# Stick-breaking attention rebuilt in units of two heads, with one PSUM bank for projection tiles

## The chip, the cores and the metric

One core of a Trainium2 chip runs one execution of a whole encoder block. The metric is device time in microseconds, lower is better. PE is the matrix engine, PEld its weight load, DVE the vector engine, ACT the scalar engine, POOL the GpSimd engine, SP the engine that here only issues DMAs. PSUM is the accumulator memory: 8 banks of 128 partitions x 512 fp32 values.

## The reference

A layer takes x (1024 tokens x 1024 features). The part that the change touches is one of two branches of the mixing sub-layer:

```
h = modulate(rmsnorm(h_res, pre_mix_g[l]), sh1, sc1)
proj = h @ w_in[l]            # q_s, k_s, v_s: 8 heads x 64 features; a_s: 1024 gate logits
z = jnp.einsum('bthd,bshd->bhts', q[:, t0:t1], k[:, :t1]) * scale
valid = s_idx[None, :] < t_idx[:, None]
log_1m = jnp.where(valid, -jax.nn.softplus(z), 0.0)
log_stick = lax.cumsum(log_1m, axis=3, reverse=True) - log_1m
a = jnp.where(valid, jnp.exp(jax.nn.log_sigmoid(z) + log_stick), 0.0)
outs.append(jnp.einsum('bhts,bshd->bthd', a, v[:, :t1]))
...
mixed = (jax.nn.sigmoid(a_r) * (ret @ w_ret_branch[l])
         + jax.nn.sigmoid(a_s) * (sb @ w_sb_branch[l]))
```

Each attention weight is thus sigmoid(z) times the product of sigmoid(-z) over all valid keys to its right. Retention, the output projection and a feed-forward layer follow. Six vectors of 1024 modulate the layer; each is silu(c) times a 1024 x 1024 matrix ("ada"). Two of them are needed at once, four later.

## The kernel before, in words

Every projection is done in three fp32r matmuls per chunk (high x high, high x low, low x high, lines 539 to 541 and 478 to 480): each operand is split into a high and a low part. The weights stream in as *pieces* of 256 columns. SP loads the two halves of a piece into `raw`; POOL splits them into `w_hi` and `w_lo` (lines 389, 391), in one of two slots, once PE has finished with what lay there; a piece is two halves.

The work before the feed-forward layer runs in stages. In the **stick stage** a loop of `STICK_G` = 2 turns does two pairs of heads each: 16 projection tiles (q and k tiles of 128 features x 512 tokens, v tiles of 128 tokens x 256 features, 8 chunks of 3 matmuls each; `stick_tile`), then `stick_pair` twice. A pair's step s takes query block i = s // 2 and head h = s % 2 of the pair, over all its (i + 1) x 128 keys at once: PE computes the scores (`scores`: 64-row operands, since a head has 64 features) into two banks and adds the mask with a matmul (L560); ACT writes sigmoid(z) to `sg` (L923) and sigmoid(-z) to `uu` (L924); DVE scans `uu` into running products from the right (L1285) and multiplies them into `sg` (L1287); PE transposes the result block by block (`weights_transposed`, L570); ACT copies it to `aT` (L929); PE multiplies with v (`times_v`, L582). v is stored with zeros beside it, so that each head's product fills 128 output partitions, its own 64 and zeros. DVE splits the result (L1292, L1294).

The order is written out by hand on each engine. On PE a step is scores(s), a part of a projection tile, transposes of step s - 2, the rest of that tile, times_v of s - 3; the table `STICK_BESIDE` says which tile stands beside which step: the first eight steps of a turn's first pair have one, the first six of its second pair too, steps after them none. Tiles of a turn's start stand alone, ahead of the pair. DVE also does the four later ada vectors there, between the scans: 64 multiply-adds over 512 columns (`ada_step`, L1267, L1269) out of `raw`, and PE sums them over partitions (`ada_row`, L592).

The **gate stage** follows, g = 0 and 1: eight tiles of 8 chunks (`piece_T`, sigmoid on ACT, L950) and eight of 4 chunks that multiply by w_sb (evicted by DVE, L1335). Then come retention, merge, output projection and feed-forward.

The changed functions of all five engines stand here as they were.

## Time and profile before

| | |
|---|---|
| runs | 1976.05, 1965.62, 1970.85 us; median 1970.85 |
| profiled execution, its own time | 1968.33 us |
| its span, first to last instruction | 1966.5 us |
| mean granted clock of PE | 0.957 of full speed |
| PE busy | 1792.9 us, 91% |
| DVE, ACT, POOL busy | 925.6, 521.7, 668.8 us |

A busy share is the share of the span in which an engine had an instruction in work. Matmuls overlap: each record is longer than the distance to the next one, so costs of PE are read from the distance between two starts. The granted clock is 1.0 at 2.4 GHz and 0.5 at 1.2 GHz. An entry such as "PE ps L570 <- DVE sg L1287" says that PE stood idle before an instruction of line 570 until DVE had finished one of line 1287.

### The profile page before, as it was taken

The page shows a single profiled execution, that of the slowest core. Times are in us where ns is not written, and L with a number is a line of the kernel's source. Part 1 is how long each engine was busy: PE and PEld are TensorE (multiplying, and loading weights), DVE is VectorE, ACT ScalarE, POOL GpSimd, SP SyncE. Part 2 cuts the span into 40 slices and gives each one's busy share as a digit, 9 for nine tenths or more (in the row PEclk, how much of TensorE's full clock was granted, in tenths as well). Part 3 has the DMA queues.
Part 4 walks back from the last instruction along what each step waited for, and adds up shares of the span by engine and source line. Part 5 has one row for each costly group of instructions (what it writes and reads, how often), then busy time and mean ns, then how long its engine had stood idle before and what let it go on. Part 6 is the DMA issues. An engine that isn't in the chain of part 4 may idle for free.

```text
span 1966.5 us, 25526 instructions
## 1 busy us (share of the span) xinstructions
PE 1792.9 (91%) x9648; PEld 1513.2 (77%) x9648; DVE 925.6 (47%) x1321; ACT 521.7 (27%) x833; POOL 668.8 (34%) x283
## 2 busy tenths in 40 slices
PE   1799889979999998999999997589999999999998
PEld 1677677767889897988788797567888888888886
DVE  6574837492105455454311326647436263453616
ACT  2333413341001212111100113342333333233332
POOL 4020132014333331313333476334543544445320
PEclk8799988999999999999999998799999999999999
DMA  8020313031113111101211144302021120211103
GB/s 313 12 97 11 96 35 107 1 97 52 46 35 140 44 38 33 44 25 43 110 62 43 43 160 141 139 33 86 22 64 43 43 68 27 75 43 43 60 31 146
DMA packets 38086, 135.15 MB, mean 69 GB/s; under 512 B 5864, under 2 KB 6760, under 8 KB 37488
## 3 DMA queue, kind: packets, MB, share of 16 engines
q1 hardware_dynamic: 30320, 109.29, 17.2%
q10 hardware_dynamic: 7680, 24.65, 3.4%
q8 instruction: 62, 1.02, 0.2%
q14 instruction: 24, 0.20, 0.0%
HBM read 121.33 MB, written 12.60 MB: 68 GB/s over the span
## 4 chain that ended last, share of the span: by engine, by line
PE 79%; DVE 12%; issue 4%; ACT 2%; POOL 2%; DMA 0%; DVEq 0%; POOLq 0%; SPq 0%; ACTq 0%
PE ps L478 15%; PE ps L479 15%; PE ps L480 15%; PE ps L820 5%; PE ps L821 5%; PE ps L822 5%; PE ps L539 3%; DVE uu L1285 3%; PE ps L540 3%; PE ps L541 3%; PE ps L582 2%; PE ps L699 1%; DVE sg L1238 1%; DVE qk L1415 1%; PE ps L570 1%
## 5 line engine op out<-in xcount | busy, mean ns | idle before, releaser
L389 POOL TENSOR_TENSOR w_hi<-raw,zero 128x1024 fp32r<-128x1024 f32 x80 | 164.9, 2062 | 833.7 <-DMA raw<-wstream 367.0
L478 PE MATMUL ps<-r_hi,w_hi 128*128 128x512 f32 x640 | 254.5, 398 | 23.1 <-issue 20.3
L479 PE MATMUL ps<-r_lo,w_hi 128*128 128x512 f32 x640 | 254.1, 397 | 0.0
L480 PE MATMUL ps<-r_hi,w_lo 128*128 128x512 f32 x640 | 252.7, 395 | 0.0
L478 PE MATMUL ps<-w_hi,a_hi 128*128 128x256 f32 x768 | 222.4, 290 | 20.6 <-DVE qkT L1421 9.1
L479 PE MATMUL ps<-w_lo,a_hi 128*128 128x256 f32 x768 | 217.6, 283 | 0.0
L480 PE MATMUL ps<-w_hi,a_lo 128*128 128x256 f32 x768 | 217.3, 283 | 0.0
L391 POOL TENSOR_TENSOR w_lo<-raw,w_hi 128x1024 fp32r<-128x1024 f32 x80 | 206.9, 2587 | 6.3
L417 POOL TENSOR_TENSOR w_lo<-w,w_hi 128x1024 fp32r<-128x1024 f32 x39 | 101.3, 2598 | 249.6 <-ACT w_hi L1070 249.6
L1551 DVE TENSOR_TENSOR m<-m,ps 128x512 f32<-128x512 f32 x224 | 146.3, 682 | 71.9 <-PE ps L822 71.6
L478 PEld LDWEIGHTS ps<-w_hi,a_hi 128*128 128x128 f32 x768 | 149.1, 194 | 23.1 <-POOL w_hi L389 10.3
L478 PEld LDWEIGHTS ps<-r_hi,w_hi 128*128 128x128 f32 x640 | 121.7, 190 | 51.2 <-issue 20.5
L820 PE MATMUL ps<-w_hi,f_hi 128*128 128x512 f32 x392 | 155.9, 398 | 4.2 <-issue 4.2
L821 PE MATMUL ps<-w_lo,f_hi 128*128 128x512 f32 x392 | 155.7, 397 | 0.0
L822 PE MATMUL ps<-w_hi,f_lo 128*128 128x512 f32 x392 | 155.5, 397 | 0.0
L480 PEld LDWEIGHTS ps<-w_hi,a_lo 128*128 128x128 f32 x768 | 148.9, 194 | 0.0
L479 PEld LDWEIGHTS ps<-w_lo,a_hi 128*128 128x128 f32 x768 | 148.6, 193 | 0.0
L480 PEld LDWEIGHTS ps<-r_hi,w_lo 128*128 128x128 f32 x640 | 121.7, 190 | 28.0
L479 PEld LDWEIGHTS ps<-r_lo,w_hi 128*128 128x128 f32 x640 | 121.7, 190 | 26.4
L1285 DVE TENSOR_TENSOR_SCAN uu<-uu 128x128 f32<-128x128 f32 (+7 forms) x64 | 100.2, 1566 | 67.7 <-ACT uu L924 67.6
L1544 DVE TENSOR_TENSOR f_lo<-hid,f_hi 128x1024 fp32r<-128x1024 f32 x35 | 48.7, 1392 | 149.0 <-ACT f_hi L1097 149.0
L417 POOL TENSOR_TENSOR w_lo<-raw,w_hi 128x1024 fp32r<-128x1024 f32 x32 | 77.6, 2433 | 99.3 <-ACT w_hi L1070 98.9
(223 smaller groups left out, 3509.2 us busy)
## 6 DMA issues: line engine op xcount, KB each, us to landing
raw<-wstream SPq DMA_DIRECT2D x112, 512.0 KB, 3.6
raw<-ada_rows SPq DMA_DIRECT2D x32, 512.0 KB, 3.5
w<-wstream SPq DMA_DIRECT2D x32, 512.0 KB, 3.5
ada_s<-ada SPq DMA_DIRECT2D x8, 1024.0 KB, 18.5
xs<-x SPq DMA_DIRECT2D x2, 2048.0 KB, 11.7
m_dram<-m1s ACTq DMA_DIRECT2D x1, 4096.0 KB, 12.5
...
```

Source lines behind the costliest of these rows:

```text
L389: nc.gpsimd.tensor_tensor(w_hi[:, slot, part], raw[:, h, :], zero[:, 0:1].broadcast_to([P, RAW]), ALU.add).then_inc(w_split, 1)
L391: nc.gpsimd.tensor_tensor(w_lo[:, slot, part], raw[:, h, :], w_hi[:, slot, part].bitcast(f32), ALU.subtract).then_inc(w_split, 1)
L417: return nc.gpsimd.tensor_tensor(out_, in0, in1, op)
L478: nc.tensor.matmul(outp, lh, rh, start=(k == 0), stop=False)
L479: nc.tensor.matmul(outp, lh, rl, start=False, stop=False)
L480: last = nc.tensor.matmul(outp, ll, rh, start=False, stop=(k == chunks - 1))
L539: nc.tensor.matmul(outp, hi, r_hi_, start=start, stop=False)
L820: nc.tensor.matmul(banks[:, t, :], fh, wh, start=(start and c == 0), stop=False, skip_group_check=not start)
L821: nc.tensor.matmul(banks[:, t, :], fh, wl, start=False, stop=False, skip_group_check=not start)
L822: last = nc.tensor.matmul(banks[:, t, :], fl, wh, start=False, stop=(c == 1), skip_group_check=not start)
L1285: V.tensor_tensor_scan(prod, prod, prod, 1.0, ALU.mult, ALU.bypass).then_inc(scan_done, 1)
L1551: V.tensor_tensor(dst, dst, bank, op).then_inc(ff_ev, 1)
```

## The change

- **Units.** The 64 head-steps become 48 *units* of both heads of a pair: query block i against at most four key blocks. Blocks 0 to 3 are one unit each, blocks 4 to 7 two: first the four blocks at the right end (`diagonal`, with the mask), then the i - 3 others, whose scan begins with the product that the first left (a copy of one column, `pad`). A pair has 12 units, its widths (keys per head) are 128, 256, 384, 512, then 512 four times paired with 128, 256, 384, 512.
- **Scores.** The six matmuls of a unit alternate between the heads: operand rows 0 to 63 and 64 to 127, written to two neighbouring banks. Banks 0, 1 and 2, 3 alternate from unit to unit.
- **One sigmoid for both heads** over two banks, sigmoid(-z) first; one copy for both heads' transposes; one multiply for both on DVE, two scans.
- **Products with v.** v has no zeros beside it. Each matmul has 64 columns of v for its stationary operand; head 0 writes output partitions 0 to 63 and head 1 writes 64 to 127 of the same bank, alternately.
- **Projection tiles.** All 32 go beside units, over all four pairs, and so do the first four gate tiles; apart from the first two they have one bank, so a tile waits until the one before it is evicted (for q and k tiles until DVE's low part). `qk_hi`, `qk_lo` are doubled.
- **PE's order in a step U**: transposes of U - 2, scores of U, tiles, times_v of U - 2.
- **Result of the products**: ACT copies it to `sbt_f` (32 copies), DVE splits it in eight wide instructions after the last unit, behind which `ada_step` and the gate tiles of 4 chunks stand.
- **Ada vectors** go from the stick stage to the gate stage, with a ring of three buffers of their own; ACT evicts and issues their rows. DVE waits for the last of these rows before retention.
- **Weight pieces** are split in straight code, each when the last tile of the piece two before it is done. The loop of two turns is gone on every engine.

Of the tables (they are 4 and 9 lines) two lines are shown. Other entries of `STICK_BESIDE` say for instance that unit 14 has chunks 3 to 7 of tile 15 (k of pair 1) and unit 15 all of tile 16 (v, second half of the heads).

```diff
+UNITS = tuple(u for i in range(T) for u in ([(i, 0, i + 1, True)] if i < 4 else [(i, i - 3, i + 1, True), (i, 0, i - 3, False)]))
+N_UNITS = len(UNITS)
+ALL_UNITS = 4 * N_UNITS
+FIRST_UNIT = tuple(k for k, u in enumerate(UNITS) if u[3])
+LAST_UNIT = tuple(k for k, u in enumerate(UNITS) if u[1] == 0)
...
+STICK_TILE = ([("q", 0, 0), ("k", 0, 0)] +
+              [("v", 0, t) for t in range(4)] + [("q", 0, 1), ("k", 0, 1), ("v", 0, 4), ("v", 0, 5), ("q", 1, 0), ("v", 0, 6), ("k", 1, 0), ("v", 0, 7)] +
...
+    0: ((2, 0, 8), (3, 0, 8)), 1: ((4, 0, 8), (5, 0, 8)), 2: ((6, 0, 8),), 3: ((7, 0, 8), (8, 0, 8)), 4: ((9, 0, 8),),
...
+            return ps[:, n, :] if n < 2 else ps[:, 7, :]
+
+        def z_banks(U, w):
+
+            return ps[:, 2 * (U % 2):2 * (U % 2) + 2, 0:w]
...
+            def ada_rows_in(lo, hi):
+
+                for m in range(lo, hi):
+                    if m >= ADA_RING:
+                        sp.wait_ge(ada_acc, m - ADA_RING + 1)
+                    sp.dma_start(ada_r[:, m % ADA_RING, :], ada_rows[m, :, :]).then_inc(ada_row_in[m % ADA_RING], 16)
+
+            for n in range(1, PC_GATE + 3):
+                piece_in(n)
+            ada_rows_in(0, 6)
+            piece_in(PC_GATE + 3)
...
+            for n, last in ((2, ("k", 0, 1)), (3, ("v", 0, 7)), (4, ("k", 1, 1)), (5, ("k", 2, 1)), (6, ("v", 1, 7)), (7, ("k", 3, 1))):
+                piece(n, n + 1, n % 2, TL_STICK + TILE_AT[last] + 1)
...
+                hi, lo = qk_hi[G % 2], qk_lo[G % 2]
+                for n, (a, b) in enumerate(((hi, hi), (lo, hi), (hi, lo))):
+                    for h in range(2):
+                        rows_ = slice(64 * h, 64 * h + 64)
+                        last = nc.tensor.matmul(z_banks(U, w)[:, h, :], a[rows_, 0, i * P:(i + 1) * P], b[rows_, 1, b0 * P:b1 * P],
+                                                start=(n == 0), stop=(n == 2 and not diagonal))
...
+                for b in range(b0, b1):
+                    for h in range(2):
+                        half = slice(h * SB_DH, (h + 1) * SB_DH)
+                        last = nc.tensor.matmul(px[half, 2, 0:P], vs[:, g, b, sub, half],
+                                                aT[:, h, (b - b0) * P:(b - b0 + 1) * P],
+                                                start=(k in FIRST_UNIT and b == b0), stop=(k in LAST_UNIT and b == b1 - 1))
...
+                    if n >= 3:
+                        pe.wait_ge(*((ev_act, EA_STICK + n) if STICK_TILE[n - 1][0] in "va" else (qk_low, LOW_AFTER[n])))
...
+            for U in range(ALL_UNITS + 2):
+                if U >= 2:
+                    weights_transposed(U - 2)
+                if U < ALL_UNITS:
+                    scores(U)
+                for n, k0, k1 in STICK_BESIDE.get(U, ()):
+                    stick_tile(n, k0, k1)
+                if U >= 2:
+                    times_v(U - 2)
...
+                if g:
+                    piece_T(n, g % 2, a_hi, a_lo, lambda j: (ev_dve, ev - 3 + j))
+                    ada_row(1)
+                    piece_T(n + 1, 1 - g % 2, a_hi, a_lo, lambda j: (ev_act, ea + j + 1))
+                    ada_row(2)
+                else:
+                    piece_T(n + 1, 1, a_hi, a_lo, lambda j: (sg_done, 2 * ALL_UNITS))
+                    pe.wait_ge(sbt_split, 8)
                 piece_T(n + 2, g % 2, sbt_hi, sbt_lo, lambda j: (ev_act, ea + j + 5) if j < 4 else (ev_dve, ev + j - 3),
                         chunks=4, cols=HALF, order=tuple((m, th) for m in range(4) for th in range(2)))
+                ada_row(3 * g)
...
+            for U in range(ALL_UNITS + 3):
+                if U >= 3 and (U - 3) % N_UNITS in LAST_UNIT:
+                    G, k = divmod(U - 3, N_UNITS)
+                    i = UNITS[k][0]
+                    act.wait_ge(av_done, T * G + i + 1)
+                    nc.scalar.activation(sbt_f[:, G, i * P:(i + 1) * P], px[:, 2, 0:P], ACT.Copy).then_inc(sbt_ready, 1)
+                if 2 <= U < ALL_UNITS + 2:
+                    _, b0, b1, _ = UNITS[(U - 2) % N_UNITS]
+                    w = (b1 - b0) * P
+                    act.wait_ge(at_tr, U - 1)
+                    nc.scalar.activation(aT[:, :, 0:w], px[:, 0:2, 0:w], ACT.Copy).then_inc(at_ready, 1)
+                if U < ALL_UNITS:
+                    _, b0, b1, _ = UNITS[U % N_UNITS]
+                    w = (b1 - b0) * P
+                    act.wait_ge(z_done, 2 * U + 2)
+                    nc.scalar.activation(uu[:, U % 2, :, HALF - w:HALF], z_banks(U, w), ACT.Sigmoid, scale=-1.0).then_inc(sg_done, 1)
+                    nc.scalar.activation(sg[:, U % 2, :, 0:w], z_banks(U, w), ACT.Sigmoid).then_inc(sg_done, 1)
+                for n, _, k1 in STICK_BESIDE.get(U, ()):
+                    if k1 == KC:
+                        high(n)
...
+            def row_out(v):
+
+                act.wait_ge(ada_mm, 2 + v + 1)
+                for hv in range(2):
+                    nc.scalar.activation(acc[0:1, v, hv, :], px[0:1, 2 * (v % 2) + hv, :], ACT.Copy).then_inc(ada_ev, 1)
+                act.wait_ge(ada_ev, 2 + 2 * v + 2)
+                act.dma_start(mods[v:v + 1, :], acc[0:1, v, :, :].rearrange("p a n -> p (a n)")).then_inc(mods_out, 16)
...
+                for h in range(2):
+                    run = uu[:, slot, h, HALF - w:HALF if diagonal else HALF + 1][:, ::-1]
+                    dve.wait_ge(sg_done, 2 * U + 1)
+                    V.tensor_tensor_scan(run, run, run, 1.0, ALU.mult, ALU.bypass).then_inc(scan_done, 1)
+                dve.wait_ge(scan_done, 2 * U + 2)
+                if k not in LAST_UNIT:
+                    V.tensor_copy(uu[:, 1, :, HALF:HALF + 1], uu[:, 0, :, 0:1]).then_inc(pad_set, 1)
+                    pads += 1
+                dve.wait_ge(sg_done, 2 * U + 2)
+                V.tensor_tensor(sg[:, slot, :, 0:w], sg[:, slot, :, 0:w], uu[:, slot, :, HALF - w + 1:HALF + 1], ALU.mult).then_inc(a_done, 1)
+                for n, _, k1 in STICK_BESIDE.get(U, ()):
+                    if k1 == KC and STICK_TILE[n][0] in "qk":
+                        low(n)
...
+            dve.wait_ge(sbt_ready, 4 * T)
+            for G in range(4):
+                V.tensor_copy(sbt_hi[:, G, :], sbt_f[:, G, :]).then_inc(sbt_split, 1)
+                dve.wait_ge(sbt_split, 2 * G + 1)
+                V.tensor_tensor(sbt_lo[:, G, :], sbt_f[:, G, :], sbt_hi[:, G, :].bitcast(f32), ALU.subtract).then_inc(sbt_split, 1)
...
+                for m in range(14, 24) if g else range(6):
+                    ada_step(m)
                 for j in range(8):
+                    ada_step((24 if g else 6) + j)
...
+            dve.wait_ge(mods_out, 16 * 4)
```

**On PE, a head-step of 640 keys before** (pair 0, block 4; a step without a tile beside it). L570 are the transposes, L582 the products with v, the others the scores, L560 the mask.

```order
L570 MATMUL ps<-id_f,sg 128x128 x4
L580 REGISTER_ALU
L582 MATMUL ps<-aT,vs 128x128 x4
L554 REGISTER_ALU
L539 MATMUL ps<-qk_hi 128x512
L540 MATMUL ps<-qk_lo,qk_hi 128x512
L541 MATMUL ps<-qk_hi,qk_lo 128x512
L539 MATMUL ps<-qk_hi 128x256
L540 MATMUL ps<-qk_lo,qk_hi 128x256
L541 MATMUL ps<-qk_hi,qk_lo 128x256
L560 MATMUL ps<-msk_b,id_b 128x128
```

And the change's unit 11 (pair 0, block 7, its four left key blocks; also without a tile). L591 are the transposes, L575 the scores of both heads, L608 the products.

```order
L608 MATMUL ps<-aT,vs 64x128 x8
L591 MATMUL ps<-id_f,sg 128x128 x6
L575 MATMUL ps<-qk_hi 128x512 x2
L575 MATMUL ps<-qk_hi,qk_lo 128x512 x2
L575 MATMUL ps<-qk_lo,qk_hi 128x512 x2
L608 MATMUL ps<-aT,vs 64x128 x6
L591 MATMUL ps<-id_f,sg 128x128 x8
```

The scores of one head have become those of two, each pass twice in a row on different halves of the rows, and the products with v are 64 wide and follow the transposes of their own unit at a distance of the scores (and of the tile, where there is one).

**On DVE before**, between two scans of pair 0 (queries of block 3), stand the ada multiply-adds and the split of the result:

```order
L1285 SCALAR_TENSOR_TENSOR uu<-uu 128x512
L1286 REGISTER_ALU
L1287 TENSOR_TENSOR sg<-sg,uu 128x512
L1290 REGISTER_ALU
L1292 ISA
L1292 COPY sbt_hi<-ps 128x128
L1293 REGISTER_ALU
L1294 REGISTER_ALU
L1294 TENSOR_TENSOR sbt_lo<-ps,sbt_hi 128x128
L1269 SCALAR_TENSOR_TENSOR acc<-raw,silu_c,acc 128x512
L1265 REGISTER_ALU
L1269 SCALAR_TENSOR_TENSOR acc<-raw,silu_c,acc 128x512
```

and the change's DVE, units 20 to 22 (pair 1, blocks 6 and 7; L1295 the scans, printed by the form of their instruction; L1301 the multiply, L1276 the low part of a q or k tile):

```order
L1295 SCALAR_TENSOR_TENSOR uu<-uu 128x512 x2
L1298 COPY uu<-uu 128x2
L1301 TENSOR_TENSOR sg<-sg,uu 128x1024
L1276 SCALAR_TENSOR_TENSOR qk_lo<-ps,qk_hi 128x512
L1295 SCALAR_TENSOR_TENSOR uu<-uu 128x385 x2
L1301 TENSOR_TENSOR sg<-sg,uu 128x2x384
L1295 SCALAR_TENSOR_TENSOR uu<-uu 128x512 x2
L1298 COPY uu<-uu 128x2
L1301 TENSOR_TENSOR sg<-sg,uu 128x1024
```

Nothing but scans, multiplies and low parts stands there now.

**On PE around unit 15 of the change**, with what each row waits for: scores and mask of unit 15, then the first matmul of tile 16, the first tile that uses piece 4.

```order
L575 MATMUL ps<-qk_hi 128x512 [waits sg_done]
L575 MATMUL ps<-qk_hi 128x512
L575 MATMUL ps<-qk_hi,qk_lo 128x512 x2
L575 MATMUL ps<-qk_lo,qk_hi 128x512 x2
L581 MATMUL ps<-msk_b,id_b 128x128 x2
L558 MATMUL ps<-w_hi,a_hi 128x256 [waits qk_low,w_split]
L559 MATMUL ps<-w_lo,a_hi 128x256
L560 MATMUL ps<-w_hi,a_lo 128x256
```

Piece 4 goes into the slot of piece 2, whose last tile is tile 15, the one directly ahead of tile 16.

## Rows read from the trace of the kernel before

**Rows 1.** The page, section 4: the whole chain by engine, share of the span.
```profile
PE 79%; DVE 12%; issue 4%; ACT 2%; POOL 2%; DMA 0%; DVEq 0%; POOLq 0%; SPq 0%; ACTq 0%
```

**Rows 2.** Stretches: us, then busy of each engine (instructions), granted clock, DMA, GB/s.
```profile
74.40:266.30 191.90, 168.55 (x1002) 139.55 (x1001) 125.00 (x151) 70.56 (x120) 32.60 (x12) 0.93 0.18 56
266.30:457.90 191.60, 170.70 (x1000) 141.28 (x1000) 119.48 (x139) 64.69 (x113) 32.52 (x12) 0.92 0.20 61
457.90:590.80 132.90, 132.90 (x585) 109.21 (x585) 12.25 (x20) 9.58 (x16) 43.37 (x21) 1.00 0.16 48
```

**Rows 3.** Waits of PE, 74 to 458 us: total us, times, longest.
```profile
PE ps L570 <- DVE sg L1287: 33.4, 17, 8.1
```

**Rows 4.** Timeline of PE, end of pair 1: start, us, line, tile, count.
```profile
247.97 1.97 PE L570 MATMUL ps<-id_f,sg 128*128 128x128 f32 x8 [8.14 <-DVE sg L1287]
...
261.32 2.00 PE L592 MATMUL ps<-acc,ones 128*1 128x512 f32 x4
266.31 0.47 PE L539 MATMUL ps<-a_hi,w_hi 128*128 128x512 f32 x1 [2.99 <-issue]
```

**Rows 5.** Timeline of DVE in that place, a scan of 1,024.
```profile
240.72 4.42 DVE L1285 TENSOR_TENSOR_SCAN uu<-uu 128x1024 f32<-128x1024 f32 x1
```

**Rows 6.** Timeline of ACT: eviction of a v tile, then of a gate tile.
```profile
91.68 0.39 ACT L909 ACTIVATE vs<-ps 128x256 f32<-128x256 f32 x1 [2.33 <-PE ps L541]
...
469.21 0.60 ACT L950 ACTIVATE m1s<-ps 128x512 f32<-128x512 f32 x1 [4.89 <-PE ps L480]
```

**Rows 7.** Timeline of PE, one head, 640 keys: scores, mask, transposes, products.
```profile
132.60 0.49 PE L539 MATMUL ps<-qk_hi 64*128 64x512 f32 x1
132.94 0.39 PE L540 MATMUL ps<-qk_lo,qk_hi 64*128 64x512 f32 x1
133.17 0.39 PE L541 MATMUL ps<-qk_hi,qk_lo 64*128 64x512 f32 x1
...
133.78 0.23 PE L560 MATMUL ps<-msk_b,id_b 128*128 128x128 bf16 x1
133.85 0.61 PE L570 MATMUL ps<-id_f,sg 128*128 128x128 f32 x4
134.29 1.06 PE L582 MATMUL ps<-aT,vs 128*128 128x128 f32 x8
135.28 0.50 PE L539 MATMUL ps<-qk_hi 64*128 64x512 f32 x1
```

**Rows 8.** Timeline of PE in retention: records of 128 rows, then of 64.
```profile
642.92 0.61 PE L721 MATMUL ps<-vr,st_sb 128*128 128x128 f32 x4
643.46 0.49 PE L725 MATMUL ps<-state,qkT 64*128 64x128 f32 x4
643.79 0.39 PE L688 MATMUL ps<-qkT 64*128 64x128 f32 x4
```

**Rows 9.** Groups by form, 74 to 458 us, DVE then ACT: busy, mean ns.
```profile
L1269 DVE SCALAR_TENSOR_TENSOR acc<-raw,silu_c,acc 128x512 f32<-128x512 f32 x56 | 50.1, 894 | 1.1
...
L1310 DVE SCALAR_TENSOR_TENSOR qk_lo<-ps,qk_hi 128x512 fp32r<-128x512 f32 x16 | 10.8, 683 | 22.7 <-ACT qk_hi L912 22.7
L1285 DVE TENSOR_TENSOR_SCAN uu<-uu 128x512 f32<-128x512 f32 x8 | 9.8, 1222 | 5.1 <-ACT uu L924 5.1
...
L1287 DVE TENSOR_TENSOR sg<-sg,uu 128x512 f32<-128x512 f32 x8 | 5.5, 691 | 0.3
...
L924 ACT ACTIVATE uu<-ps 128x1024 f32<-128x1024 f32 x8 | 8.2, 1019 | 0.0
```

**Rows 10.** Groups of POOL, 72 to 458 us: busy, mean ns.
```profile
L391 POOL TENSOR_TENSOR w_lo<-raw,w_hi 128x1024 fp32r<-128x1024 f32 x12 | 35.4, 2954 | 0.9
...
L389 POOL TENSOR_TENSOR w_hi<-raw,zero 128x1024 fp32r<-128x1024 f32 x12 | 29.8, 2487 | 338.6 <-DMA raw<-wstream 338.6
```

**Rows 11.** Nine stretches of PE at the low clock: the third, and the sum.
```profile
242.80:253.00 10.20, 4.96 (x22) 0.50 0.39 127
...
sum 54.50, PE 42.67; mean PE 4.74
```

403 lines of the change are left out of this document (156 added, 247 removed), and 7 rows, old and new, of the table STICK_BESIDE.

## The prediction, made before the changed kernel ran

> **What bounds the kernel now.** I read the chain of waits first: PE carries 79% of it, DVE 12% [rows 1]. So a change pays where it shortens PE's own work or a wait of PE. Then the stretches of the stages the change touches [rows 2]: the stick stage runs from 74.4 to 457.9 us, 383.5 us, and PE is busy 168.6 + 170.7 = 339.3 of them: it stands idle 44.2 us. The gate stage behind it is solid PE, 132.9 of 132.9 us. In the stick stage 33.4 us of the idle time stand before the transposes, which wait for DVE's multiply, 17 times [rows 3]. The longest such wait, 8.1 us, is at the end of a pair [rows 4], where no projection tile stands beside the heads, and where a scan of 1,024 took 4.42 us [rows 5] while POOL split weights; 1.22 us for 512 [rows 9] would let one expect 2.4. After such waits the granted clock is at 0.50, the 1.2 GHz level, for 3.4 to 10.2 us: nine stretches, 54.5 us in all, with 42.7 us of PE work in them [rows 11], which cost half of that, 21 us.
>
> **Prices on PE**, from distances between starts at full clock. A q, k or gate tile (24 matmuls): 0.60 + 4.89 = 5.49 us from eviction to eviction; a v tile: 0.39 + 2.33 = 2.72 us [rows 6]. A score pass of 512 keys 0.23 us, the first one 0.34, so 0.11 for the entry; mask 0.07; one transpose 0.44 / 4 = 0.11 us; products with v 0.99 us for four blocks of one head, eight records [rows 7]. Four ada records 2.0 us [rows 4].
>
> Check on the stage before: 16 x 5.49 + 16 x 2.72 = 131.4; scores 216 passes of 512 x 0.23 + 64 x 0.18 = 61.2; 288 transposes 31.7; 288 blocks of products 71.3; ada rows 4 x 2.0 = 8.0. Sum 303.6, with 44.2 idle and 21 for the clock 369. The other 14 us (5% of the work) are short matmuls that cost more than their share.
>
> **The change, part by part.**
>
> *Scores.* Two heads alternate on the two halves of the rows. Retention already does this: four records on all 128 rows took 643.46 - 642.92 = 0.54 us, four on alternating halves 0.33 us [rows 8], which is two pairs at 0.11 and an entry of 0.1. So the halves run side by side. 108 passes x 0.23 + 48 entries x 0.11 + 32 masked units x 0.15 = 34.9 instead of 61.2 us. Bounds: 34.9, and 24.8 more if fp32r passes (retention's are fp32) do not pair.
>
> *Products with v.* The halves are now halves of the output partitions, one bank. No row shows that. Bounds: all of it serial, 71.3 us, or paired, 35.7. I take 35.7, because the nearest row [rows 8] pairs. The Trainium skill, TensorEngine Tiling (Array Packing), section Theoretical Speedup, allows up to twice the rate for 64 columns or fewer; no run here shows it.
>
> *Change of array shape.* Going from full rows to half rows cost 0.11 us [rows 7], once a unit in my sum. The Trainium skill, same page, section Key Properties, says that a change of tiling mode drains the engine. With products in half columns a unit has four changes of shape, 192 in all; at the row's 0.11 each the other 144 would add 16 us. My sum leaves them out since the row behind the scores (L560) and the transposes show no such gap; it is a rival below.
>
> *Tiles.* 16 + 4 x 5.49 and 16 x 2.72: 153.3 us; the four gate tiles (22.0) leave the gate stage. Transposes 31.7 as before.
>
> PE's work: 153.3 + 34.9 + 31.7 + 35.7 = 255.6, with 4% for short forms 265 us.
>
> *Waits of PE left in the stage.* (a) Scores of unit 0 wait for the low part of k: drain 0.2 + 0.60 + 0.68 [rows 6, 9] = 1.5. (b) One tile bank: v after v within a unit waits for drain and eviction, 0.6, twice; a tile behind a q or k tile within a unit (units 3, 13, 25, 37) 1.5; where DVE does the low part only behind its own scans, three or four times up to 2. Together 13. (c) Piece 4: it is split only when tile 15 is done, and tile 16 is the next one. A piece is 2 x (2.49 + 2.95) = 10.9 us on POOL [rows 10]; between the two tiles PE has about 1.6 us of other work: 9.3. Pieces 2 and 5 have 11 to 12 us of PE work in between, and the others more: nothing, or 2 each if DVE slows POOL. (d) After unit 47: sigmoid 1.02, two scans 2.44, multiply 1.4, copy 1.02 against some 3 us of PE work: 3.3. Sum 27.
>
> *Clock.* The 9.3 us wait should be followed by 10.2 us at the low level as in rows 11, this time full of tiles: 5; the short waits another 4. Sum 9.
>
> Stage: 265 + 27 + 9 = 301 us, for 383.5.
>
> *DVE, ACT, POOL.* Per pair DVE has 18 x 1.22 of scans, 18 x 0.69 of multiplies, four low parts of 0.68 [rows 9]: 37 us, 150 for four pairs, at most 33 more if every microsecond of the six pieces halves it. ACT: three instructions a unit, nine times 1.02 each per pair [rows 9]: 110 us, with evictions and 32 small copies 140. Both lie beside PE's 265. Within a unit of 512 with half a tile PE has about 5.7 us, DVE 3.9: PE stays last. If the pairing failed, PE would only be further behind.
>
> *Gate stage.* 132.9 - 22.0 + 8.0 (ada rows) = 118.9. DVE gets 64 multiply-adds here, 0.89 us each [rows 9], 57 us, plus 16 multiplies of 0.69 and the split of the result (eight instructions of 1,024, at most 2 x 0.69 each, 11 us): about 79 in 119. Nothing on the path: the split has four tiles (22 us) before the first use. It would cost where a 2.75 us tile stands against 1.8 + 0.69 of DVE while POOL works; three banks of lead, 8 us, cover the 5 us of delay. Without them 5 us per turn. On SP the ada loads stand behind the piece loads and these behind POOL's splits; three rows are in flight before DVE starts, and a turn has 44 us for at most 18 rows: 0, or a few us. Retention starts with DVE waiting for the last ada row: sum, copy, DMA, some 5 us, against four tiles of 2.72 in four banks: 0. The loop's return (2.99 us, [rows 4]) was in the idle time.
>
> **Sum.** 301 + 118.9 against 383.5 + 132.9: -96.5 us. The profiled execution took 1968.33 us: 1871.8. The median of the runs is 2.5 us above it; I say **1873**.
>
> **The rivals.**
> 1. *Products do not pair.* +36 us of PE work, of which some 5 fill waits: 1904. For: no row for column halves, both write one bank. Against: rows 8. Chance 0.2.
> 2. *Shape changes cost on every side.* +16: 1889. The Trainium skill's drain rule (above) would give this; the trace has the entry and not the way back. Chance 0.1.
> 3. *Scores do not pair*, alone or with the products: 1898 or 1927. Chance 0.05.
> 4. *Slower: alternating halves drain each other.* If each of 288 score and 576 product records had to wait out the tail of the one before (0.39 long at a distance of 0.23: 0.16), that is +138 on top of the 61 for no pairing: 2070. It decides from (96.5 - 61) / 864 = 0.04 us per record. Rows 8 speak plainly against it for rows, nothing does for columns. Chance 0.03.
> 5. *Weights and low parts stall PE more than I count* (pieces 2 and 5, POOL slowed by scans, bank 7 behind DVE): +15: 1888. Chance 0.12.
> That the change does no work that it removes is excluded by the order of the instructions; only the clock could take the gain back, by 20 at most.
>
> **How the numbers follow.** Main case 0.5, 1873, itself 1855 to 1890 (waits 15 to 35, clock 4 to 15, short forms 0 to 15). The range 1850 to 1908 takes in rivals 1, 2 and 5. Faster by over 0.5% (about what a measurement can tell from no change): all cases but the fourth and a part of the unknown, 0.95; same 0.02; slower 0.03.
>
> **What would show it.** In the new profile: scores of both heads starting in pairs a few ns apart, products too (if their records lie 0.12 apart one by one, rival 1); stick stage near 301 us and gate near 119; one wait of PE of about 9 us before tile 16, put down to POOL; no long wait on DVE's multiply except at the end; POOL idle elsewhere; DVE busy in the gate stage without holding PE. It is wrong if the stage takes over 335 us, or if PE waits for DVE or ACT in most units.

## The result, and the profile after

The changed kernel takes 1919.12 us (median of 4 runs, 1917.12 to 1925.92), the kernel before in the same job 1968.39 us. The ratio is 0.975, with a 95% interval from 0.9711 to 0.9788: 49 us faster. The forecast was 1873 us, 96.5 us faster, with a range of 1850 to 1908. The direction was right, the size was not: half of the gain is missing, and the time lies outside the range. Of the runs of e3_rows below, one (2048.67 us, at a granted clock of 0.83 against 0.95 to 0.96 in the others) was in a slower state of the chip and is left out of its median.

The profiled execution took 1925.92 us, 6.8 us above its median, so the sums below, made on it, come to 54 us missing and not 46. The three stretches of [rows 2], the last one reaching to the end, in the new trace (window, length in us, then busy of each engine with its instructions, granted clock, DMA share, GB/s):

```profile
74.60:398.60 324.00, 290.14 (x2066) 224.43 (x2064) 183.18 (x188) 139.79 (x216) 73.47 (x28) 0.96 0.08 25
398.60:531.60 133.00, 125.22 (x513) 93.64 (x513) 89.43 (x88) 10.64 (x19) 47.99 (x20) 0.95 0.47 159
531.60:1924.10 1392.50, 1320.54 (x6977) 1116.32 (x6976) 617.45 (x939) 354.19 (x551) 526.25 (x221) 0.97 0.19 65
```

and PE in the last one before, from the first matmul of retention, which is at 589.9 and not at 590.8 where the prediction cut (us, PE busy, clock, DMA share, GB/s):

```profile
589.90:1966.50 1376.60, 1301.12 (x6977) 0.97 0.20 66
```

So the 54 us stand in three places: the stick stage takes 324.0 us where 301 were forecast (+23), the gate stage 133.0 for 118.0 (+15; the forecast's 118.9 held 0.9 us of retention), and everything behind it, which the change does not touch, 1392.5 for 1376.6 (+16). The last one is the surprise: PE is busy for 19 us more with the same 6977 matmuls. (3.5 of these 16 us are the granted clock: PE was busy at the 1.2 GHz level for 42.6 us there and for 35.7 before, and half of the difference is time.)

The waits of PE in the first two stretches (total us, times, longest):

```profile
PE ps L591 <- DVE sg L1301: 12.7, 5, 5.9
PE ps L558 <- POOL w_lo L412: 8.4, 1, 8.4
PE ps L558 <- DVE qk_lo L1276: 8.0, 7, 1.5
PE ps L654 <- DVE acc L1328: 7.8, 1, 7.8
PE ps L608 <- ACT aT L937: 2.3, 2, 1.2
PE ps L575 <- DVE qk_lo L1276: 1.4, 1, 1.4
PE ps L558 <- ACT vs L917: 1.1, 2, 0.6
```

L591 is the transposes, L558 the first pass of a projection tile, L654 the ada rows, L608 the products, L575 the scores. The 33.4 us of [rows 3] have become 12.7; the wait for POOL is the one forecast before tile 16. The wait of L654 is the one in the gate stage, and was forecast as nothing; the others are 33.9 us in the stick stage.

One step in the timeline of PE at full clock: the end of the products, transposes, scores of both heads, masks, the first two passes of half a tile; then its last pass, the products and the next transposes.

```profile
282.37 0.61 PE L608 MATMUL ps<-aT,vs 128*64 128x128 f32 x8
282.91 1.09 PE L591 MATMUL ps<-id_f,sg 128*128 128x128 f32 x8
283.93 0.51 PE L575 MATMUL ps<-qk_hi 64*128 64x512 f32 x2
284.27 0.40 PE L575 MATMUL ps<-qk_hi,qk_lo 64*128 64x512 f32 x2
284.50 0.39 PE L575 MATMUL ps<-qk_lo,qk_hi 64*128 64x512 f32 x2
284.82 0.28 PE L581 MATMUL ps<-msk_b,id_b 128*128 128x128 bf16 x2
284.92 0.47 PE L558 MATMUL ps<-a_hi,w_hi 128*128 128x512 f32 x1
285.23 0.39 PE L559 MATMUL ps<-a_lo,w_hi 128*128 128x512 f32 x1
...
287.56 0.40 PE L560 MATMUL ps<-a_hi,w_lo 128*128 128x512 f32 x1
287.89 1.09 PE L608 MATMUL ps<-aT,vs 128*64 128x128 f32 x16
288.92 0.44 PE L591 MATMUL ps<-id_f,sg 128*128 128x128 f32 x2
```

Two things are to be seen. Both heads' scores of 512 keys take 0.89 us from the first to the mask (284.82 - 283.93), and both heads' products of four blocks 1.03 us (288.92 - 287.89), where one head alone took 0.99 [rows 7]: the heads seem to run side by side. And at each change of array shape something is lost on both sides: the first score pass is 0.34 from the next where the second is 0.23; the last of the three stands 0.32 before the mask; the first pass of the tile 0.31 before the second, where 0.23 is usual; the tile's last pass 0.33 before the products. In the trace of before the same can be read around [rows 7], where I read only the entry, 132.60 to 132.94. The next head's scores, at 135.28, stand 0.20 us behind the last product, where two products are 0.11 apart; and the last score pass,

```profile
133.57 0.27 PE L541 MATMUL ps<-qk_hi,qk_lo 64*128 64x128 f32 x1
```

stands 0.21 us before the mask (133.78), where two such passes are 0.11 apart.

In all, over the 48 units, the median excess at such places is 0.15 us from products to transposes, 0.20 from transposes to scores, 0.21 from scores through the mask to the tile, 0.14 from the tile to the products: 0.70 us a unit, 34 us in the stage. (A change can be preceded or followed by a change of data type here, of the bf16 mask above all; the 0.70 holds both.)

The work of PE by kind bears this out. Each record is counted to the start of the next one, without the waits, and time at the 1.2 GHz level is halved:

| PE work, us | before, by the check | before, in the trace | changed, forecast | changed, in the trace |
|---|---|---|---|---|
| Projection tiles | 131.4 | 138.7 | 153.3 | 166.3 |
| Scores and masks | 61.2 | 70.1 | 34.9 | 39.2 |
| Transposes | 31.7 | 31.3 | 31.7 | 38.5 |
| Products | 71.3 | 69.6 | 35.7 | 38.1 |
| Ada rows, in the changed kernel "short forms" | 8.0 | 7.7 | 9.4 | |
| Sum | 303.6 | 317.4 | 265 | 282.1 |

### The profile page after: what moved, and what is told of

It is laid out like the page before. It is cut to its first block, busy times and chain, and to the rows that moved or that the text cites. A ratio compares the mean times of both kernels' runs of the same rounds, so it can differ in the third digit from the quotient of the medians.

```text
span 1924.1 us, 24724 instructions
## 1 busy us (share of the span) xinstructions
PE 1758.3 (91%) x9648; PEld 1453.6 (76%) x9648; DVE 942.4 (49%) x1291; ACT 529.1 (27%) x822; POOL 667.4 (35%) x282
## 4 chain that ended last, share of the span: by engine, by line
PE 81%; DVE 11%; issue 3%; POOL 2%; ACT 2%; DMA 0%; POOLq 0%; DVEq 0%; SPq 0%; ACTq 0%
PE ps L497 15%; PE ps L499 15%; PE ps L498 15%; PE ps L829 5%; PE ps L831 5%; PE ps L830 5%; PE ps L558 3%; PE ps L559 2%; PE ps L560 2%; PE ps L591 2%; PE ps L575 2%; PE ps L608 1%; DVE uu L1295 1%; PE ps L708 1%; DVE sg L1256 1%
## 5 line engine op out<-in xcount | busy, mean ns | idle before, releaser
L1295 DVE TENSOR_TENSOR_SCAN uu<-uu 128x512 f32<-128x512 f32 (+7 forms) x96 | 105.1, 1136 | 118.4 <-ACT uu L942 118.1
L499 PEld LDWEIGHTS ps<-r_hi,w_lo 128*128 128x128 f32 x640 | 121.1, 189 | 29.0
## 6 DMA issues: line engine op xcount, KB each, us to landing
ada_s<-ada SPq DMA_DIRECT2D x8, 1024.0 KB, 18.5
m<-m_dram ACTq DMA_DIRECT2D x1, 4096.0 KB, 12.4
```

The source lines that it names most:

```text
L499: last = nc.tensor.matmul(outp, ll, rh, start=False, stop=(k == chunks - 1))
L1295: V.tensor_tensor_scan(run, run, run, 1.0, ALU.mult, ALU.bypass).then_inc(scan_done, 1)
```

## The experiments

All are edits of the changed kernel unless another is named, and each time is a median of 4 to 10 runs. "Of a0" means against the changed kernel's 1920.61 us in the first of these jobs; kernels of different jobs are compared over it, which is good to some 3 us, the before of the jobs lying between 1968 and 1974. A difference of under 5 us needs the profile too, as the next section shows.

### The changed kernel again (a0_same)

No edit.

> The changed kernel once more, unaltered, as the common measure of these runs. Two theories on the missing 47 us: (A) it is in the change itself, some 23 us in the stick stage and 14 us in the gate stage, and the profiled execution (1925.92 us) was also one in which all the code behind it, which nobody touched, ran about 0.8% slower; (B) the change makes the later stages slower by some lasting effect, about 10 us. By A the time is 1918 to 1920 again, and a profile whose time is near 1918 shows the stages from retention to the end within 3 us of the 1375.7 us of before. By B they take 1385 us or more in every profile.

Measured 1920.61 us (1917.64 to 1925.22), profile 1920.58 us. From retention to the end the profiled execution took 1390.4 us:

```profile
528.40:1918.80 1390.40, 1317.41 (x6977) 0.98 0.19 65
```

(A) falls for this part: the later stages are slower by 14 us, more than the 10 of (B).

Part of such a time is the granted clock, which differs between executions of the same instructions. From the first matmul of retention to the end, with PE's busy time at the 1.2 GHz level inside it and the time less half of that, in us:

| Run | retention to the end | busy at the 1.2 GHz level | less half |
|---|---|---|---|
| before | 1376.6 | 35.7 | 1358.8 |
| changed, first profile | 1392.5 | 42.6 | 1371.2 |
| a0_same | 1390.4 | 34.1 | 1373.4 |
| e1_av_serial | 1386.3 | 25.3 | 1373.7 |
| e7_scores_first | 1386.8 | 26.7 | 1373.4 |
| e4_gate | 1385.5 | 26.0 | 1372.5 |
| e5_piece4 | 1387.3 | 26.9 | 1373.8 |
| e10_before_shifted | 1387.5 | 27.9 | 1373.6 |
| e6_silu_in_tiny | 1375.7 | 33.7 | 1358.8 |
| e13_shift64 | 1389.3 | 36.9 | 1370.9 |
| e14_shift128 | 1389.5 | 45.5 | 1366.8 |
| e15_shift256 | 1377.0 | 41.8 | 1356.2 |

The clock moves this part by up to 10 us from one profile to another. So what an edit of the stick or the gate stage is worth is read from the length of that stage, and a difference of a few us between whole times says little by itself.

### Addresses (e6_silu_in_tiny, e10_before_shifted, e13_shift64, e14_shift128, e15_shift256)

The instructions of the later stages are the same in both kernels. What differs is where their tiles lie: `silu_c`, 8 words per partition, moved ahead of them.

```diff
-        silu_c = sb("silu_c", [P, KC], f32)
         tiny = sb("tiny", [P, 96], f32)
+        silu_c = tiny[:, 80:88]
```

> The change moves a vector of 32 bytes per partition (silu of c) out of the stage's own memory to a place ahead of nearly all other tiles, so that every tile behind it, those of retention, output and feed-forward too, lies 32 bytes further on. Here the vector lives in free columns of an old tile, and all later stages have their addresses of before again. Theory B' (the addresses make the unchanged later stages 10 us slower: steady passes with the low part of the weights stand 0.237 us apart and not 0.229): the time falls by 8 to 16 us against the unaltered changed kernel, and the part from retention to the end takes 1367 to 1372 us between the first and the last matmul and not 1376 to 1383. Rival (a later phase of queues and transfers, or the chip's mood): 0 to 3 us.

Measured 1903.34 us (1902.63 to 1908.5), 17 us less, ratio to before 0.9673 (0.9652 to 0.9695). The kernel before got the hole instead:

```diff
+        sb("shift", [P, KC], f32)
         tiny = sb("tiny", [P, 96], f32)
```

> The kernel before with 32 bytes per partition left empty at the same place, nothing else. Theory B': it becomes 8 to 16 us slower than before (and a little more if the tiles of the stick stage suffer too), with the low-part passes at 0.237 us. Rival: within 3 us of before.

Measured 1985.07 us against 1968.23, ratio 1.0084 (1.0063 to 1.0106): 17 us more. The stretch from retention to the end, first of e6_silu_in_tiny, then of e10_before_shifted:

```profile
525.80:1901.50 1375.70, 1298.11 (x6977) 0.98 0.20 65
```

```profile
591.20:1978.70 1387.50, 1314.26 (x6977) 0.98 0.20 65
```

With the vector out of the way it is the 1376.6 us of before, and with the hole 11 more, or 15 with the clock taken off (table above). PE's busy time follows, 1301 and 1298 against 1314 to 1321. From start to start, the passes of 512 columns between `r_hi`/`r_lo` and the weights in the last 660 us (some 1,430) stand on average 0.2307 us apart in the kernel before and 0.2290 with the vector in the old tile, and 0.2333 in the changed kernel and in the kernel before with the hole; the feed-forward's second passes 0.2333 in the first two, 0.2342 in the others. So it is each matmul that runs 0.4 to 1.9% slower, not some wait. The low-part distance of 0.237 us is as expected, the 0.229 is 0.232 in e6_silu_in_tiny, where the high-part passes gained instead (0.226 for 0.231); why the kernel before and e6_silu_in_tiny differ in this way was not looked for. Other distances were tried by a longer hole behind the vector, 32, 96 or 224 bytes:

> The changed kernel with another 32 bytes left empty behind the moved vector, so that every later tile lies 64 bytes further on than in the kernel before, and not 32. If alignment to 64 bytes is what matters, the loss is gone: 1903 us, as with the vector in an old tile. If the distance itself or the new neighbours matter: 1915 to 1921 us.

> The changed kernel with 96 more bytes left empty behind the moved vector: every later tile lies 128 bytes further on than in the kernel before. If places count modulo 128 bytes: 1903 us. If any move loses the old speed, or if it goes by a larger step: 1915 to 1923 us.

> The same with 224 more bytes, so a move of 256. If places count modulo 256 (and not modulo 128): 1903 us here and over 1915 with 128. If both are slow, no step up to 256 brings it back, and the rule stays open.

Measured 1922.55 us at 64 bytes (1920.13 to 1925.1), 1917.93 at 128 (1915.2 to 1920.74), 1901.68 at 256 (1899.72 to 1906.44), where retention to the end took 1377.0 us. So it is not alignment to 64 or 128 bytes; at 256 the old speed is back, in full. With 0 and 256 fast and 32, 64 and 128 slow, a rule modulo 256 bytes fits the five distances. It is not all: at 128 the later stages lose 8 us and not 12 to 15 by the table above, the rest of that run's time being clock. `w_hi`, `w_lo` and `raw` are allocated ahead of the vector and lie still in every one of these kernels; so for these passes what moves is the activations, as against the weights. Which of their tiles, or which neighbour, it is was not looked for.

### The price of a change of shape (e3_full, e3_cols, e3_rows)

```diff
                     last = passes(tile_bank(n)[:, 0:256 if kind == "v" else HALF], *l, *r_, k == 0, k == KC - 1)
+                    if kind == "v" and k < 7:
+                        nc.tensor.matmul(tile_bank(n)[0:64, HALF - P:HALF], id_b[:, 0:64], msk_b[:, :], start=False, stop=False)
```

That is e3_cols; e3_full has all 128 rows and columns of `id_b`, e3_rows the first 64 rows of both operands.

> Price of a change of array shape by itself. In each of the 16 v tiles a small extra matmul (bf16, 128 columns moved, onto columns of the bank that nobody reads) stands behind each of the first seven chunks: 112 in all. Here it uses the full array, 128 rows by 128 columns, like its neighbours: no change of shape. By every theory 112 x about 0.06 us = 7 us more than the unaltered changed kernel, somewhat more if short weights show.

> The same 112 extra matmuls, but with 64 output columns: the shape changes to half columns and back at each. Theory A (a change of shape costs 0.14 to 0.2 us, for half columns as for half rows, on the way in and on the way back): 224 changes, 31 to 45 us more than e3_full. Rival (only the entry costs, 0.11 us, as the prediction counted): 12 us more. Rival (half columns change nothing, the gaps in the profile come from waiting for the copies of the weights): 0 to 2 us more.

> The same 112 extra matmuls, with 64 rows of weights and of data and all 128 output columns. Theory A: as e3_cols, 31 to 45 us more than e3_full. Rival (only the entry costs): 12 us more.

Measured 1936.32 us (1932.89 to 1939.41), 1971.34 (1960.73 to 1982.33) and 1972.05 (1963.91 to 1981.69). One chunk of a v tile with its neighbours, at full clock, first of e3_full, then of e3_cols (the extra matmul is L636):

```profile
148.68 0.23 PE L636 MATMUL ps<-msk_b,id_b 128*128 128x128 bf16 x1
148.72 0.36 PE L558 MATMUL ps<-w_hi,a_hi 128*128 128x256 f32 x1
148.92 0.28 PE L559 MATMUL ps<-w_lo,a_hi 128*128 128x256 f32 x1
149.04 0.28 PE L560 MATMUL ps<-w_hi,a_lo 128*128 128x256 f32 x1
149.16 0.23 PE L636 MATMUL ps<-msk_b,id_b 128*128 128x128 bf16 x1
```

```profile
148.29 0.24 PE L636 MATMUL ps<-msk_b,id_b 128*64 128x128 bf16 x1
148.47 0.39 PE L558 MATMUL ps<-w_hi,a_hi 128*128 128x256 f32 x1
148.69 0.28 PE L559 MATMUL ps<-w_lo,a_hi 128*128 128x256 f32 x1
148.81 0.28 PE L560 MATMUL ps<-w_hi,a_lo 128*128 128x256 f32 x1
149.01 0.24 PE L636 MATMUL ps<-msk_b,id_b 128*64 128x128 bf16 x1
```

A chunk alone takes 3 x 0.117 = 0.35 us, with the full extra matmul 0.48, with the half one 0.72. The time of e3_cols is 35 us above e3_full, that of e3_rows 36: over 224 changes 0.16 us each. At full clock it is (0.72 - 0.48) / 2 = 0.12. The difference between the two is the granted clock. The first v tiles at the same place, in e3_full, then in e3_cols (us, PE busy, clock, DMA share, GB/s):

```profile
89.60:130.60 41.00, 38.36 (x258) 0.96 0.04 14
```

```profile
89.60:130.60 41.00, 39.87 (x142) 0.50 0.00 0
```

In the profiles up to 700 us PE was busy at the 1.2 GHz level for 34 us in e3_full, 71 in e3_cols and 73 in e3_rows; half of the 37 more, 18.5, are clock in the 43 us between the profiles of e3_full and e3_cols, and the other 24.4 are 0.11 a change. The executions of e3_cols with the highest granted clock (0.963, 1960.73 and 1961.73 us) are some 27 us above those of e3_full with 0.964 to 0.966: 0.12. So a change costs 0.12 us here, and the rest of the 35 us, with the spread of 20 us from run to run, is the clock (0.963 at 1961 us, 0.948 at 1982). Half columns and half rows cost alike. The two rivals with 12 or 0 us fall. The full one cost 16 us and not 7: 0.13 to 0.14 us for a matmul that moves 128 columns, more than the 0.06 us of its data (0.117 / 2). It is bf16 between fp32r passes, and the pass behind it stands 0.20 before the next and not 0.117; that the data type is the reason was not tested by itself.

### Is it really paired? (e1_av_serial, e2_scores_serial, e8_one_half)

```diff
-                for b in range(b0, b1):
-                    for h in range(2):
+                for h in range(2):
+                    for b in range(b0, b1):
```

> Products with v: all blocks of one head, then all of the other, instead of block by block in turn; same instructions, same shapes, same number of changes of shape. Theory A (the two column halves run side by side, and what is lost is lost in changes of shape and in waits): 288 blocks at 0.103 us instead of 144 pairs at 0.103, so 30 us of work more in the stage, and 25 to 30 us on the time of a0_same. Rival (the halves hardly overlap and the start times of the records only look so): 0 to 5 us.

> Scores: the three passes of one head, then the three of the other, instead of in turn. Theory A (row halves run side by side): a pass of 512 columns is 0.22 us, 36 units at 512 columns and 12 at 128 to 384: 3 x (36 x 0.22 + 12 x 0.12) = 28 us more, less 5 us where it fills waits: 22 to 28 us. Rival (pairing of fp32r passes is only apparent): 0 to 5 us. If changing the row half from one matmul to the next cost something by itself, it would show here as less than 22.

e2 swaps the two loops over passes and heads in the same way. Measured 1924.13 and 1921.09 us: +3.5 and +0.5 us of a0. Taken alone this would say that pairing is worth nothing, and both expectations of my theory failed. The profiles say otherwise. In e2_scores_serial the scores read

```profile
284.38 0.50 PE L575 MATMUL ps<-qk_hi 64*128 64x512 f32 x2
284.71 0.40 PE L575 MATMUL ps<-qk_hi,qk_lo 64*128 64x512 f32 x2
284.94 0.40 PE L575 MATMUL ps<-qk_lo,qk_hi 64*128 64x512 f32 x2
285.28 0.28 PE L581 MATMUL ps<-msk_b,id_b 128*128 128x128 bf16 x2
```

The two first passes start together although the second head's is the fourth in the program. TensorE started a later matmul by itself where its half of the array was free, and for scores nothing was unpaired. For products it is otherwise: PE's work on them is 52.6 us in e1_av_serial and 39.0 in a0_same, and the stick stage ends 7.8 us later (405.6 for 397.8), since 5.6 us of waits were filled; the whole time shows only 3.5 because the clock gave back 4 us behind it (table above). So the two edits unpair nothing or under half, and an edit was needed that leaves no other half:

```diff
-                        rows_ = slice(64 * h, 64 * h + 64)
+                        rows_ = slice(0, 64)
-                        last = nc.tensor.matmul(px[half, 2, 0:P], vs[:, g, b, sub, half],
+                        last = nc.tensor.matmul(px[0:64, 2, 0:P], vs[:, g, b, sub, half],
```

> Price of the pairing. Both heads' scores are taken from the rows of the first head, and both heads' products are written to the first head's half of the output partitions (one sum of both, the second half is not written): the same number of matmuls of the same size, but none can run beside another. The second head's scores and products are not computed. Theory A (pairing works in both, and order does not matter since TensorE starts a later matmul on the free half by itself): scores 28 us more, products 144 blocks x 0.109 x 2 less what they now take, 30 us more, together 50 to 58 us more than the unaltered changed kernel, less 5 that fill waits. Rival (pairing was never worth much, which is why the two serial orders cost only 0 and 3.5 us): 0 to 10 us.

Measured 1961.6 us (1960.28 to 1969.79), +41 us. Products of four blocks of both heads, in e8_one_half and in e1_av_serial:

```profile
310.38 1.96 PE L608 MATMUL ps<-aT,vs 128*64 128x128 f32 x16
```

```profile
285.69 1.58 PE L608 MATMUL ps<-aT,vs 128*64 128x128 f32 x16
```

1.96 us one by one, 1.58 with one head behind the other on two halves, 1.09 in turn. Pairing works for scores and products. In the stage, PE's work rose from 36.0 to 61.8 us on scores and from 39.0 to 69.6 on products, 56 in all, and the waits fell from 33.9 to 21.3. It is worth 41 us on the time, less than the 45 to 53 expected, since 13 us and not 5 of the unpaired work fell into waits. The rival with 0 to 10 us falls.

### One change of shape fewer a unit (e7_scores_first)

```diff
+                if U < ALL_UNITS:
+                    scores(U)
                 if U >= 2:
                     weights_transposed(U - 2)
-                if U < ALL_UNITS:
-                    scores(U)
```

> Within each unit the scores stand ahead of the transposes of the unit two before, instead of behind them: now products, scores, mask, transposes, tile follow each other, and the transposes, which use the full array, stand beside the mask and the tile. Changes of shape per unit: three instead of four (two ends of half-shape work fall together). Theory A (a change costs 0.16 to 0.18 us whatever its kind): 46 fewer, 7 to 8 us less than the unaltered changed kernel, and up to 3 more where the scores now fill a wait for the multiply. Rival (going from half columns straight to half rows costs as much as two changes, or the later sigmoid puts new waits before the transposes): 0 to 2 us less, or slower.

Measured 1918.64 us (1917.76 to 1919.33), 2 us less. PE is busy for 282.3 us from 74.6 to 398.0, where a0_same has 289.5: the 7.2 us of work are gone, 0.16 for each of 46 changes. By kind it is the transposes that fell, from 38.6 to 31.2 us. The waits took them back: the stick stage ends at 399.0 us, and at 397.8 in a0_same, and the 2 us are no gain of the edit but clock behind it (1386.8 us for 1390.4 from retention on). The largest waits of a0_same are 12.7 (L591), 8.0 (L558 for the low part) and 2.3 us (L608), as in the first profile; those of e7_scores_first:

```profile
PE ps L558 <- DVE qk_lo L1276: 13.3, 7, 2.3
PE ps L591 <- DVE sg L1301: 10.7, 8, 2.4
PE ps L608 <- ACT aT L937: 5.8, 6, 1.1
```

The saving of work is confirmed and the gain in time is not: the one tile bank waits 5.3 us more for VectorE's low parts, and the products, with only the tile between them and their transposes, 3.5 us more for the copy.

### The gate stage (e4_gate)

```diff
+            ada_rows_in(26, 32)
             piece_in(PC_GATE + 6)
-            ada_rows_in(26, 32)
...
-                for m in range(14, 24) if g else range(6):
+                for m in range(14, 32) if g else range(6):
                     ada_step(m)
                 for j in range(8):
-                    ada_step((24 if g else 6) + j)
+                    if not g:
+                        ada_step(6 + j)
```

> Gate stage only: in the second turn VectorE does all 18 remaining ada rows before the first gate multiply instead of eight of them between the multiplies, and SyncE loads the last six rows ahead of the last weight piece. Theory A (the stall of 7.75 us before the last ada row and the 10.2 us at the low clock behind it come from ada steps that run beside GpSimd's last split and behind a late load): both go, 7.75 + 5 = 10 to 13 us less than a0_same, and the gate stage takes about 121 us. Rival (VectorE simply has too much work in the stage, 57 us of ada steps, and the wait moves to an earlier gate tile): 0 to 4 us less.

Measured 1909.1 us (1906.19 to 1913.22), 11.5 us less. From the end of the stick stage to retention it is 9.5 us (121.1 for 130.6 in a0_same); more of the whole difference is clock behind the stage (table above). The stage takes 120.5 us, all of it busy:

```profile
398.10:518.60 120.50, 120.50 (x496) 91.30 (x495) 79.52 (x88) 10.49 (x19) 38.65 (x17) 0.99 0.50 171
```

What it mended is in the timelines of the changed kernel, DVE, then PE:

```profile
482.03 0.75 DVE L1328 SCALAR_TENSOR_TENSOR acc<-ada_r,silu_c,acc 128x512 f32<-128x512 f32 x1
500.77 0.69 DVE L1341 TENSOR_TENSOR m1s<-ps,m1s 128x512 f32<-128x512 f32 x1 [17.98 <-PE ps L499]
501.37 1.53 DVE L1328 SCALAR_TENSOR_TENSOR acc<-ada_r,silu_c,acc 128x512 f32<-128x512 f32 x2
...
523.50 4.52 DVE L1328 SCALAR_TENSOR_TENSOR acc<-ada_r,silu_c,acc 128x512 f32<-128x512 f32 x2
527.95 0.68 DVE L1341 TENSOR_TENSOR m1s<-ps,m1s 128x512 f32<-128x512 f32 x1
```

```profile
528.08 3.57 PE L654 MATMUL ps<-acc,ones 128*1 128x512 f32 x4 [7.75 <-DVE acc L1328]
```

VectorE waited 18 us for the first tile to multiply, with ada work left, and then did two steps between multiplies. While GpSimd split pieces (509.3 to 530.2 us, with one pause of 1.6), two steps took 3.0 to 4.6 us and not 1.5; turns of 3.6 to 5.1 us stood against tiles of 2.8, and the last ada row came 7.75 us late. The granted clock was at 0.50 for 10.2 us from 523.3 on, in which PE was busy for 5.5. The edit took both suspects away at once, the steps beside GpSimd and the late loads of their rows; how the gain divides between them was not tested.

### The piece of weights before tile 16 (e5_piece4)

```diff
-               [("q", 1, 1), ("k", 1, 1), ("v", 1, 0), ("q", 2, 0), ("v", 1, 1), ("k", 2, 0), ("v", 1, 2), ("v", 1, 3)] +
+               [("q", 1, 1), ("k", 1, 1), ("q", 2, 0), ("k", 2, 0), ("v", 1, 0), ("v", 1, 1), ("v", 1, 2), ("v", 1, 3)] +
```

with the tiles' places in the units from 15 to 21 moved to fit.

> The order of six projection tiles alone: q and k of the third pair, first half, whose weights are split long before, stand ahead of the first v tile that needs weight piece 4, so that 11 us of tiles and not 1.6 us lie between the tile that frees the slot and the first use. Theory A (the 8.4 us wait before that v tile is GpSimd's split, and 6.8 + 3.4 us at the low clock follow from it): the wait goes to 0 to 2 us, and the time is 8 to 12 us less than the unaltered changed kernel's. Rival (VectorE and the copies are near their limit there, so that the wait moves to the units behind it): 0 to 4 us less.

Measured 1916.96 us (1914.4 to 1919.63), 4 us less, and 5 by the ratios to before (0.9731 for 0.9758). The wait of 8.36 us for POOL is gone; one of 2.70 for a low part has come, before tile 17, since a q and a k tile now follow each other in the one bank:

```profile
205.06 0.47 PE L558 MATMUL ps<-a_hi,w_hi 128*128 128x512 f32 x1 [2.70 <-DVE qk_lo L1276]
```

That is the upper edge of the rival's 0 to 4. The stick stage ends 2.7 us earlier than in a0_same (395.1 us): its waits are 4.8 us less, and PE was busy for 4.6 us more at the 1.2 GHz level.

### Together, and a version that beats both (e9_three, e11_spread, e12_spread_swap)

> Three repairs together on the changed kernel: the vector in an old tile (measured -17 us), the gate stage's ada rows ahead of the multiplies (-11.5), the order of tiles before piece 4 (-4). If they are independent: 1920.6 - 32.5 = 1888 us, between 1885 and 1892. If one hides another: over 1893.

Measured 1890.35 us (1886.35 to 1893.48), ratio 0.9587: the three repairs add up. e11_spread also moves tiles to where the units had none:

```diff
-    12: ((14, 0, 5),), 13: ((14, 5, 8), (15, 0, 3)), 14: ((15, 3, 8),),
+    11: ((14, 0, 4),), 12: ((14, 4, 8),), 13: ((15, 0, 5),), 14: ((15, 5, 8),),
...
-    42: ((33, 4, 8),), 43: ((34, 0, 4),), 44: ((34, 4, 8),), 45: ((35, 0, 4),), 46: ((35, 4, 8),)}
+    43: ((33, 4, 8),), 44: ((34, 0, 4),), 45: ((34, 4, 8),), 47: ((35, 0, 4),), 48: ((35, 4, 8),)}
```

> The three repairs, and the tiles of the stick stage spread so that the last unit of each pair and the two steps after the last unit have half a tile, where they had none: units 11, 23, 35 and steps 47, 48. In the trace of the changed kernel 2.9 us are waited before the transposes in two of these places, 1.5 us three times for the low part between two tiles that share the one bank, and 8.2 us at the end. If those waits are places where TensorE has nothing to do beside a chain of VectorE that is otherwise hidden, 8 to 12 us go: 1876 to 1880 us. If VectorE is the bound of those stretches, they turn up elsewhere: 1885 to 1890.

> As e11_spread, with the scores ahead of the transposes in each unit (46 changes of shape fewer, 7 us less TensorE work). If the waits that took that back in e7_scores_first were those of the units without a tile: 4 to 7 us less than e11_spread. If VectorE and the copies bind in most units: 0 to 2 us less.

e11_spread took 1878.21 us (1874.32 to 1886.66), ratio 0.9527 (0.9487 to 0.9567): 94 us faster than before, 42 faster than the changed kernel. Its first two stretches are 308.9 and 117.1 us:

```profile
74.60:383.50 308.90, 289.39 (x2087) 224.82 (x2088) 182.80 (x190) 141.01 (x217) 69.72 (x27) 0.97 0.08 26
383.50:500.60 117.10, 117.10 (x495) 90.30 (x493) 83.30 (x88) 10.38 (x18) 42.41 (x19) 1.00 0.52 176
```

e12_spread_swap, with the scores first, took 1881.64 us (1881.14 to 1885.28), no less. So the saving of shape changes is eaten even where nearly every unit has a tile. The waits for low parts in the one bank, and for the copies, stand right behind PE's work.

## Why the prediction was wrong, point by point

| Term | forecast | measured | shown by |
|---|---|---|---|
| Scores and products side by side | yes | yes, 41 us on the time | rows of both heads, e8_one_half |
| Changes of shape in the stick stage | 5.3, 9.4 of "short forms", some 4 inside the products | 34 | 0.70 a unit; e3_cols, e3_rows, e7_scores_first |
| Waits in the stick stage | 27 | 33.9 | the waits |
| Clock in the stick stage | 9 | 7 | busy 14.5 us at the 1.2 GHz level after 76.2 us |
| Gate stage | 118.0 | 133.0, of it 9.5 mendable | e4_gate |
| All behind it | 0 | +16: 12.4 of slower passes, 3.5 of clock | e6_silu_in_tiny, e10_before_shifted; the clock table |

Three steps failed, by some 15 us each, and the waits were 7 us more; none of these alone would have taken the time out of the range.

**Changes of shape: the first step that failed.** It is the check on the stage before, "The other 14 us (5% of the work) are short matmuls that cost more than their share", and the 4% made from it. The table of work by kind shows where these 14 us stood: 7.3 in the tiles and 8.9 in scores and masks, on whose sides the shape changes. In the trace of before the last score pass of 512 columns stands 0.32 before the mask, and the first pass of a tile behind the mask 0.32 before the second, where 0.23 is usual. They do not grow with the work but with the number of changes, which goes from 128 to 192, and four a unit at 0.175 are 34 us. Of these the sum had 5.3 as entries, 9.4 as short forms and some 4 unseen in the price of products, whose 0.99 us is 7 x 0.112 and a last distance of 0.205 to the next scores. So 15 were missing. The tiles' passes are 3 to 4 us more, at 0.232 for 5.49 / 24 = 0.229, most of it by the addresses (the tiles' work is 166.6 us in a0_same and 164.0 in e6_silu_in_tiny). Together they are about the 17 to 18 us of PE work. Rival 2 named the mechanism with 16 us on top, about what it cost, and a chance of 0.1. Its dismissal, that "the row behind the scores (L560) and the transposes show no such gap", was a misreading of [rows 7]: between mask and transposes there is no change of shape. The gap is ahead of the mask, and the row that shows it was not among the rows. The Trainium skill, TensorEngine Tiling (Array Packing), section Key Properties, says that changing the tiling mode drains the engine. The runs agree so far as every change costs 0.1 to 0.2 us, on the way in and on the way back.

**Pairing.** The choice of 35.7 for the products, "because the nearest row [rows 8] pairs", held, for columns in one bank too. Rivals 1, 3 and 4 fall. The Trainium skill, TensorEngine Tiling (Array Packing), section Theoretical Speedup, gives up to twice the rate for a dimension of 64 or less; the rows show 1.96 / 1.09 = 1.8 for products.

**Waits.** (a) was forecast at 1.5 and is 1.4; (b) at 13 and is 9.1; (c) at 9.3 and is 8.4, in its place; (d) at 3.3 and is 8.2. The end was mis-sized: the last unit's two scans were taken at 2.44 us and its multiply at 1.4, from rows at 1.22 and 0.69 us for 512, and they took, beside GpSimd's split of a gate piece (382.8 to 394.4 us),

```profile
386.62 5.65 DVE L1295 TENSOR_TENSOR_SCAN uu<-uu 128x513 f32<-128x513 f32 x2 [0.41 <-ACT uu L942]
392.31 3.18 DVE L1301 TENSOR_TENSOR sg<-sg,uu 128x1024 f32<-128x1024 f32 x1
```

Not foreseen at all: 2.9 us each before the transposes of units 11 and 35, which have no tile beside them, and 0.5 each before those of 27 and 39. In e11_spread the waits for the multiply are 5.9 us in all, for 12.7.

**Gate stage.** "Nothing on the path" failed. The text named the danger, a tile of 2.75 us against VectorE's step while GpSimd works, and set a lead of three banks against it; but the last ada row has no bank of lead, it waits for the last step itself, and the two multiply-adds of a turn took up to 4.6 us and not 1.8.

**What lies behind.** The sum sets only 301 + 118.9 against 383.5 + 132.9, and so puts all that follows at a difference of nothing, without a reason. That cost 16 us here. The whole diff shows the cause: `silu_c` leaves the stage's own memory and stands ahead of most other tiles.

The parts: 18 us of PE work and 7 of waits less 2 of clock in the stick stage, 15 in the gate stage, 16 behind: 54, as found. The addresses have some 17 of them: 12.4 behind (3.5 more there are clock) and the rest in the two stages. Rival 5 (weights and low parts stall 15 more) did not happen in its own places.

What stays open: why 256 bytes, and which operand; why the clock of untouched code differs between executions; and whether a second tile bank would let fewer changes of shape pay, which was not tried.
